# Means of five normalisations taken in four column groups of TensorE, copied once and added up by one product

## The reference

```python
def layer_norm(x, g, b):
    xf = x.astype(jnp.float32)
    mu = jnp.mean(xf, -1, keepdims=True)
    var = jnp.mean(jnp.square(xf - mu), -1, keepdims=True)
    return ((xf - mu) * lax.rsqrt(var + LN_EPS) * g + b).astype(x.dtype)
...
for l in range(DEPTH):
    ...                      # mixing sub-layer; at l = 1: u, vv = odd_in(...), layer_norm inside
    xp = layer_norm(ALPHA * xp + mix_p, ln_g[l, 0], ln_b[l, 0])
    xp = layer_norm(ALPHA * xp + cross_attn(...), ln_g[l, 1], ln_b[l, 1])
    xp = layer_norm(ALPHA * xp + moe(...), ln_g[l, 2], ln_b[l, 2])
```

## Time and profile before

| | |
|---|---|
| three runs | 1455.68 us median (1453.15 to 1456.09) |
| the profiled execution | 1461.6 us, of which the span of the trace is 1459.8 us |
| TensorE busy | 1200.5 us, 82% of the span |
| mean granted TensorE clock | 0.912 of full |
| VectorE / ScalarE / GpSimd busy | 27% / 23% / 16% |

### The profile page before, as it was taken

The page is one execution under the profiler, slowest core; times in us unless marked ns, Lnnn a source line. Parts: engine busy times, 40 slices in busy tenths (PEclk is TensorE's granted clock), DMA queues, the critical chain, the costliest instruction groups (busy, mean ns, idle before and its releaser), DMA issues.

```text
span 1459.8 us, 27239 instructions
## 1 busy us (share of the span) xinstructions
PE 1200.5 (82%) x10800; PEld 794.0 (54%) x10801; DVE 400.8 (27%) x1111; ACT 329.1 (23%) x594; POOL 233.8 (16%) x405
## 2 busy tenths in 40 slices
PE   6998888999989959755897998989988789758960
PEld 4676555567747825422454576767657445424530
DVE  0124637322423312111121402331414312111215
ACT  0005521211302212211122312011303222212321
POOL 2006990000000011111122100000000112111232
PEclk9999988999999989988898999799998899978985
DMA  9646689633556099999973953033656799999721
GB/s 327 222 150 207 203 288 388 221 115 123 224 202 231 8 397 397 398 397 396 396 274 124 380 181 115 4 115 115 219 185 258 294 399 381 348 396 397 286 61 50
DMA packets 158912, 360.31 MB, mean 247 GB/s; under 512 B 9607, under 2 KB 9623, under 8 KB 158842
## 3 DMA queue, kind: packets, MB, share of 16 engines
q1 hardware_dynamic: 145954, 331.50, 61.9%
q0 software_dynamic: 12752, 27.69, 5.5%
q10 hardware_dynamic: 144, 0.26, 0.0%
HBM read 341.47 MB, written 18.38 MB: 247 GB/s over the span
## 4 chain that ended last, share of the span: by engine, by line
PE 65%; SPq 12%; DMA 8%; DVE 8%; issue 3%; ACT 3%; POOL 0%; POOLq 0%; DVEq 0%; ACTq 0%
PE acc L670 38%; SPq L648 11%; PE psS L670 11%; PE psV L670 5%; DMA ring<-in_w_exp_down 4%; PE psN L670 4%; DVE feats L1365 2%; PE acc L964 2%; DMA feats<-in_w_exp_down 1%; PE acc L773 1%; DMA ring<-in_w_in_even 1%; PE psN L1067 1%; ACT feats L1963 1%; DMA ring<-in_w_xkv 1%; ACT arena L1241 1%
## 5 line engine op out<-in xcount | busy, mean ns | idle before, releaser
L670 PE MATMUL acc<-feats,ring 128*128 128x288 f32 x1280 | 320.5, 414 | 10.8 <-ACT feats L1883 4.2
L670 PEld LDWEIGHTS acc<-feats,ring 128*128 128x128 f32 x1280 | 247.8, 194 | 82.2 <-issue 9.8
L670 PE MATMUL psS<-ring,feats 128*32 128x256 f32 x2368 | 159.9, 430 | 76.4 <-issue 76.4
L2080 POOL DMA_DIRECT2D by_slot<-feats x208 | 103.6, 498 | 523.7 <-DVE feats L1724 278.8
L670 PEld LDWEIGHTS psS<-ring,feats 128*32 128x32 f32 x2368 | 83.8, 124 | 141.5 <-issue 104.8
L670 PE MATMUL psS<-arena,feats 128*32 128x256 f32 x1216 | 84.4, 430 | 34.1 <-issue 33.6
L1716 DVE TENSOR_TENSOR feats<-feats,psS 64x256 f32<-64x256 f32 x52 | 22.1, 425 | 316.1 <-ACT feats L1972 316.1
L1241 ACT ACTIVATE arena<-acc 128x1024 f32<-128x1024 f32 (+7 forms) x98 | 72.2, 758 | 113.5 <-PE acc L670 35.2
L1972 ACT ACTIVATE feats<-psS 64x256 f32<-64x256 f32 x52 | 19.6, 377 | 339.6 <-PE psS L670 339.6
L670 PE MATMUL psN<-arena,feats 128*32 128x256 f32 (+1 forms) x1360 | 82.1, 375 | 3.5 <-DVE feats L1689 3.5
L670 PEld LDWEIGHTS psS<-arena,feats 128*32 128x32 f32 x1216 | 41.3, 123 | 67.5 <-issue 49.6
(11 more groups left out here) (323 smaller groups left out, 1303.4 us busy)
## 6 DMA issues: line engine op xcount, KB each, us to landing
ring<-in_w_exp_gate SPq DMA_DIRECT2D x22, 2048.0 KB, 18.6
ring<-in_w_exp_up SPq DMA_DIRECT2D x22, 2048.0 KB, 22.2
ring<-in_w_exp_down SPq DMA_DIRECT2D x22, 2048.0 KB, 19.9
arena<-in_w_exp_gate SPq DMA_DIRECT2D x10, 2048.0 KB, 19.4
arena<-in_w_exp_up SPq DMA_DIRECT2D x10, 2048.0 KB, 22.6
feats<-in_w_exp_down SPq DMA_DIRECT2D x10, 2048.0 KB, 19.9
ring<-in_cache_k SPq DMA_DIRECT2D x64, 256.0 KB, 3.1
ring<-in_cache_v SPq DMA_DIRECT2D x64, 256.0 KB, 3.1
```

The source lines that it names most:

```text
L670: return pe.matmul(out, lhsT, rhs, start=first, stop=last)
L2080: pool.dma_start(by_slot[rows, 256 * q:256 * q + 256], YS[32 * q:32 * q + 32, at]).then_inc(S.stored, 16)
```

## The change

`mean_tile` is replaced for the five means by `mean_by_quarters`. It uses only 32 columns of `ones_d` per product, so that product k needs a quarter of the array's columns and writes 32 partitions, 32*(k%4) on. Products 0 to 3 start four sums and products 4 to 7 add to them. One DVE instruction, first thing in `center`, copies the bank to SBUF (`std`, not in use at that time) times 32; one product of the full `ones_d` with it adds the four partial sums: each stands on 32 partitions, so the sum over 128 partitions of 32 times the values, over 1024, is their sum. The mean then lies on all 128 partitions as before, and the rest is unchanged. Each of the five gets one more tile in the list (`mean0p` and so on, emptied by DVE). The four variances of the same normalisations, the variance of the gated unit and the convolution's mean and variance keep `mean_tile`.

```diff
@@ tile_order
+            add("vmeanp", 1, "v")
             add("vmean", 1, "v")
...
+        add(f"mean{3 * l}p", 1, "v")
         add(f"mean{3 * l}", 1, "v")
...
+        add(f"mean{3 * l + 1}p", 1, "v")
         add(f"mean{3 * l + 1}", 1, "v")
@@ tensor engine
+            def mean_by_quarters(stage, zz, ready):
+
+                bank_free(pe, stage + "p", 0)
+                for k in range(8):
+                    ready(k)
+                    q = 32 * (k % 4)
+                    last = mm(ACC(stage + "p", 0)[q:q + 32, 0:NTOK], ones_d[:, 0:32], zz[:, k, :], k < 4, k >= 4)
+                last.then_inc(acc_full, 1)
+                evacuated(pe, stage + "p", 0)
+                bank_free(pe, stage, 0)
+                mm(ACC(stage, 0)[:, 0:NTOK], ones_d[:, :], std[:, :], True, True).then_inc(acc_full, 1)
...
-                mean_tile(f"mean{3 * l}", zT, ones_d[:, :], 8, lambda k: evacuated(pe, f"o{l}", k))
+                mean_by_quarters(f"mean{3 * l}", zT, lambda k: evacuated(pe, f"o{l}", k))
...
-                mean_tile(f"mean{nth}", zT, ones_d[:, :], 8, lambda k: evacuated(pe, f"xo{l}", k))
+                mean_by_quarters(f"mean{nth}", zT, lambda k: evacuated(pe, f"xo{l}", k))
...
-                    mean_tile("vmean", vT, ones_d[:, :], 8, lambda k: evacuated(pe, "vv", k))
+                    mean_by_quarters("vmean", vT, lambda k: evacuated(pe, "vv", k))
@@ vector engine
             def center(stage, zz, n, done, step):
 
+                if n == 8:
+                    full(dve, stage + "p", 0)
+                    dve.tensor_scalar(std[:, :], ACC(stage + "p", 0)[:, 0:NTOK], 32.0, None, ALU.mult)\
+                        .then_inc(emptied["v"], 1)
                 full(dve, stage, 0)
```

## The result

The changed kernel took 1437.6 us (median of 6 runs, 1435.4 to 1441.24), the kernel before 1454.41 us beside it (6 runs, 1441.2 to 1462.29): a ratio of 0.9895, 95% interval 0.9849 to 0.9941. The first question is whether the direct gain was mis-sized or something came on top.

What follows compares the result with a forecast made beforehand. TensorE's serial work or transfers bind by stage; at the five means it is TensorE's products. -7.0 us direct + 1.0 clock = -6.0, from 1455.7 to 1449.7 us; range 1446.5 to 1454.0.

Steps and rivals of the forecast that it cites:

- What bounds the five places, and the direct cost: At the five means `center` waits for TensorE's eight serial products; 4.15 us falls to 2.72, 7.0 us in all.
- The change of shape at no cost: Regrouping TensorE's columns around the narrow products: at most 0.1 us, nothing charged, ends 0 and 0.2 us a stage.
- The shifted list: Moved pads before cross-attention's first scores: +0.4 us in layer 0, -0.4 us in layer 1, nothing in the sum.
- Carried to the end: TensorE sets both layers' expert stream starts, so all gain reaches the end; loads 2.8 and some 6 us earlier.
- Rival 2: Expert streams hide the gain: in full 1455.7 us, chance 0.10; layer 0's alone 1452.5, half of it within a shared 0.16.
- Rival 3: At the five means the narrow products do not run side by side: +6.3 us, 1462.0 us, chance 0.04.
- The clock: Variances behind `vmean` and `mean3` run at 1.2 GHz in about half of executions: 1.0 us lost, ends 0 and 3.4.
- The base: Whole kernel: the profiled 1461.6 us lies 5.9 above its runs' median, so the forecast starts from 1455.7 us.

## Why the prediction was right and wrong

- **What bounds the five places, and the direct cost: right.** `center` 2.70 us after the first product against 2.72, eight narrow products to the copy in 1.40 against 1.46, 7.3 us against 7.0. The copy took 457 to 458 ns against 0.46 us.
- **The change of shape at no cost: right.** The full product began 0.51 us behind the copy and `center` 0.79 us behind that, as costed (0.51 and 0.75); a cost of regrouping that is not hidden under the waits would have made the chain of 2.72 us longer, and it took 2.70. By TensorEngine Tiling, "Key Properties", of the Trainium skill a drain is due there; no row here shows it outside the waits.
- **The shifted list: right,** +0.4 and -0.4 us, and the kernel with the list alone shows both.
- **Carried to the end: right.** Rival 2 fell: from the first load to the last product of layer 0's experts 282.4 us before and 281.9 after, from the load to the end in layer 1 305.2 and 305.1. The first load came 6.2 us earlier where I had 2.8; 3.0 of it was there before `mean0`. The second came 20.1 us earlier where I had some 6: 7.3 direct, the same 3.0, and the rest the clock's.
- **Rival 3 fell:** 16 narrow records in 1.29 us, so four abreast.
- **The clock: wrong, and this is the step that failed.** I wrote "Ends: 0 and 3.4 us, taken 1.0", a loss or nothing. The loss exists, but in 2 of 8 profiles with quarters at `vmean` the variance ran low, for 1.5 us, and not in half. What I left out is the gain: the earlier trace rows showed the stretches at 462.30 and 979.20 at 1.2 GHz and I counted them as fixed. In the profiled pair the first of them vanished (1.5 us), the second shrank (1.1 us), the segment behind `mean4` lost 1.6 us and the cross-attention's end 0.7, together 4.9 us; and the 48 gated products, which I had not looked at, took the fast way, worth 5.2 us with the projection behind them. By the table above the first came with all 8 shortened means (and 2 of 10 unchanged ones), the second with 7 of 8 and the third with 6 of 9; the 48 products were fast only in part of the executions. Median against median: 15.5 us (1455.2, and 1439.7 over 12 runs of the changed kernel) less 7.3 is 8.2 us from the clock (6.5 by the line through the runs' own clocks), where my term had a loss of 1.0. The five products show that behind `mean1`, `mean3` and `mean4` it needs only the shift; for the 48 products no run shows what it needs.
- **The base.** I scaled to the median of three runs, 1455.7; the 100 runs have 1455.2. That was no error, but a range of -9.2 to -1.7 us was too narrow for a kernel whose own executions differ by 20 us, as 1461.6 against 1453.15 already hinted.

**Open:** what sets the share of executions in which the 48 products run fast. Quarters (3 of 5 profiles) against the same shift by five products (0 of 3) differ; filling the copy's pause did not separate them, and these 8 profiles are few and not of like executions. The fast way came in 5 of 5 profiles with the seven unread products. Why the three profiles with five wide products have the slowest, and whether their faster executions have it too, is not known. Open too is where the low clock goes when more pauses are filled.

## What to carry to other kernels

A chain of short products, a drain and a handover can be costed from rows of other stages to some hundredths of a us (2.72 for 2.70). The granted clock cannot be left at its old places: list every stretch in which TensorE is busy at 1.2 GHz (here 164.7 us), since each can vanish or move when the work ahead of it shifts by 1.4 us, and put a gain of that kind in the range. Where every run's mean granted clock is on record, set the times against it before explaining a difference: here that parts the direct gain from the clock's. Where pauses of some microseconds stand ahead of dense small products, a few unread products in the pause are a cheap trial (7 us here on the kernel before); more of them in later pauses brought nothing more that shows.

## What the runs showed of the hardware

TensorE stayed at 1.2 GHz through 13.7 us of unbroken work with 128-column products (48 records, clock 0.50), and ran the same 48 records in 7.8 us in other executions. Executions of one program differ by 21 us (1441.1 to 1462.3), and the time goes with the mean granted clock (12.1 us for 0.01). One place where it arises: between two profiles of the kernel before, 31.9 and 25.4 us for the same 93 records round the sampled rows' attention. The two kernels that leave part of all five means out had one more turn of experts and took some 7.5 us longer there; the two that do so at `vmean` alone did not. A left-out computation need not be neutral where data choose the work.
